# Four banks instead of two for a head's value tiles in the gated mixer and in retention

## What is computed

```python
q, k = silu(causal_dwconv(mq)), silu(causal_dwconv(mk))      # gated mixer only
# gated mixer, per head: a = decay weights exp(...) times (q . k) / 16
num_t = sum_{s<=t} a[t,s] * v[s]
den_t = max(|sum_{s<=t} a[t,s]|, exp(-m_t))
h_t   = num_t / den_t
hm    = sigmoid(mo) * head_rms(h)
# retention, per head:
o_t   = sum_{s<=t} gamma^(t-s) * (q_t . k_s) * v_s
hr    = silu(rg) * head_rms(o)
y     = gm * (hm @ w_mlstm_out) + gd * (hd @ w_diff_out) + gr * (hr @ w_ret_out)
```

## Time and profile before

| | |
|---|---|
| median of 3 runs | 2582.63 us (2580.34 to 2588.62) |
| the profiled execution | 2586.39 us, its span 2584.6 us |
| TensorE busy, share of the span | 2470.8 us, 96% |
| VectorE, ScalarE, GpSimd busy | 1088.5, 891.9, 186.5 us |
| mean granted TensorE clock | 0.976 of full |
| DMA | 219.96 MB, 85 GB/s |

### The profile page before, as it was taken

The page is one execution under the profiler, slowest core; times in us unless marked ns, Lnnn a source line. Parts: engine busy times, 40 slices in busy tenths (PEclk is TensorE's granted clock), DMA queues, the critical chain, the costliest instruction groups (busy, mean ns, idle before and its releaser), DMA issues.

```text
span 2584.6 us, 29079 instructions
## 1 busy us (share of the span) xinstructions
PE 2470.8 (96%) x11448; PEld 2021.8 (78%) x11448; DVE 1088.5 (42%) x1383; ACT 891.9 (35%) x1403; POOL 186.5 (7%) x252
## 2 busy tenths in 40 slices
PE   7999999999989999997999999999999999899997
PEld 7666788887877888886777788888877787788886
DVE  3444533445565443345444322223246534433334
ACT  3442422323443332234433423332245533522222
POOL 3000500002002200001000000000000000100001
PEclk9989999999989999998999999999999999999999
DMA  5611332232211323232222232222331123232221
GB/s 149 87 55 59 115 98 97 97 97 81 91 41 49 115 97 97 97 97 65 66 79 67 82 98 82 81 82 84 100 82 50 50 85 103 73 99 96 98 98 65
DMA packets 187040, 219.96 MB, mean 85 GB/s; under 512 B 20531, under 2 KB 141568, under 8 KB 186832
## 3 DMA queue, kind: packets, MB, share of 16 engines
q1 hardware_dynamic: 183200, 206.13, 25.2%
q0 software_dynamic: 3760, 12.73, 2.3%
HBM read 213.60 MB, written 5.24 MB: 85 GB/s over the span
## 4 chain that ended last, share of the span: by engine, by line
PE 91%; DVE 4%; ACT 2%; POOL 1%; issue 1%; DMA 0%; SPq 0%; POOLq 0%; ACTq 0%; DVEq 0%
PE A L471 46%; PE B L471 42%; DVE WL L1533 1%; DVE Y L1657 1%; ACT WH L1037 0%; DMA X<-in_x 0%; PE C L721 0%; ACT Y L1130 0%; ACT ar L1040 0%; PE C L946 0%; DVE st L1645 0%; POOL st L2137 0%; PE C L787 0%; POOL st L2123 0%; PE C L641 0%
## 5 line engine op out<-in xcount | busy, mean ns | idle before, releaser
L1533 DVE TENSOR_TENSOR WL<-RAW,WH 128x2048 fp32r<-128x2048 f32 (+1 forms) x197 | 450.4, 2286 | 753.1 <-ACT WH L1037 753.1
L1037 ACT ACTIVATE WH<-RAW 128x2048 fp32r<-128x2048 f32 (+1 forms) x197 | 376.0, 1909 | 666.9 <-PE A L471 601.7
L471 PE MATMUL B<-XH,WH 128*128 128x512 f32 x1360 | 538.6, 396 | 1.4 <-DVE XL L1543 1.4
L471 PE MATMUL B<-XL,WH 128*128 128x512 f32 x1360 | 531.6, 391 | 0.0
L471 PE MATMUL B<-XH,WL 128*128 128x512 f32 x1360 | 531.2, 391 | 0.0
L471 PE MATMUL A<-WH,YH 128*128 128x512 f32 (+1 forms) x976 | 377.8, 387 | 3.4 <-DVE YL L1592 1.8
L471 PE MATMUL A<-WL,YH 128*128 128x512 f32 (+1 forms) x976 | 377.1, 386 | 0.0
L471 PE MATMUL A<-WH,YL 128*128 128x512 f32 (+1 forms) x976 | 377.1, 386 | 0.0
L471 PEld LDWEIGHTS B<-XH,WH 128*128 128x128 f32 x1360 | 256.8, 189 | 70.4 <-issue 15.2
L471 PEld LDWEIGHTS B<-XH,WL 128*128 128x128 f32 x1360 | 256.6, 189 | 54.2
L471 PEld LDWEIGHTS B<-XL,WH 128*128 128x128 f32 x1360 | 257.0, 189 | 51.7
(11 more groups left out here) (272 smaller groups left out, 2106.4 us busy)
## 6 DMA issues: line engine op xcount, KB each, us to landing
RAW<-in_w_in SPq DMA_DIRECT2D x33, 1024.0 KB, 5.2
RAW<-in_mlp_w_up SPq DMA_DIRECT2D x32, 1024.0 KB, 5.4
RAW<-in_mlp_w_down SPq DMA_DIRECT2D x32, 1024.0 KB, 5.0
RAW<-in_w_in SPq DMA_DIRECT2D x48, 512.0 KB, 4.3
RAW<-in_w_ffn_in SPq DMA_DIRECT2D x22, 1024.0 KB, 5.0
RAW<-in_w_ffn_out SPq DMA_DIRECT2D x10, 1024.0 KB, 5.1
RAW<-in_mla_w_o SPq DMA_DIRECT2D x4, 1024.0 KB, 5.0
RAW<-in_swa_w_q SPq DMA_DIRECT2D x4, 1024.0 KB, 4.9
```

What stands on the lines that cost most here:

```text
L471: return nc.tensor.matmul(dst, l, r, start=first, stop=last)
L1037: nc.scalar.activation(WH[s][:, 0:n], RAW[s][:, 0:n], ACT.Copy).then_inc(hi_ready, 1)
L1533: tt(WL[s][:, 0:n], RAW[s][:, 0:n], f32(WH[s][:, 0:n]), ALU.subtract).then_inc(lo_ready, 1)
```

## The change

Two uses of B per head become uses of C. Tiles 0 and 1 stay in B0 and B1; tiles 2 and 3 go to the two C banks, and the two transposed tiles follow them in C. Since n0 is odd (85 and then 101), tile 2 gets C1 and tile 3 C0, and the transposed tiles C1 and C0, as before. ScalarE's drain and VectorE's copy of the denominator name the bank by the same function, and each frees the bank's own semaphore. A head now counts three uses of each B bank (before four) and two of each C bank (before one), so all wait numbers in the two stages change: the features that follow in B wait for tile 0's and tile 1's drain where they waited for tile 2's and tile 3's. The order of the instructions on every engine stays. The diff, cut to its core (the second PLAN line and the callers change in the same way):

```diff
-    ("ml", 16, 12, 32, 8, 4, 8),
+    ("ml", 16, 12, 24, 16, 4, 8),
-    ("ret", 16, 8, 32, 8, 4, 8),
+    ("ret", 16, 8, 24, 16, 4, 8),
+    def head_bank(name, t):
+        _, _, rb, n0, _, _ = BASE[name]
+        if t < 2:
+            return B[t], b_free[t], rb // 2 + 2, 3
+        u = n0 + t - 2
+        return C[u % 2], c_free[u % 2], u // 2, 2
+
+    def head_out(name, m):
+        u = BASE[name][3] + 2 + m
+        return C[u % 2], c_free[u % 2], u // 2, 2
...
-        def head_transposed(name, i, n0, src):
+        def head_transposed(name, i, src):
             pe.wait_ge(s_(name + "_h"), T * i + T)
             for m in range(2):
-                b = (n0 + m) % 2
-                pe.wait_ge(c_free[b], (n0 + m) // 2 + i)
+                bank, free, n, per = head_out(name, m)
+                pe.wait_ge(free, n + per * i)
                 for t in range(T):
-                    r = nc.tensor.transpose(C[b][:, tok(t)], src[:, t, tok(m)], ident[:])
+                    r = nc.tensor.transpose(bank[:, tok(t)], src[:, t, tok(m)], ident[:])
...
-        def decayed_values(name, i, rounds, rb, at, v, width):
+        def decayed_values(name, i, rounds, at, v, width):
             for t in range(T):
+                bank, free, n, per = head_bank(name, t)
                 pe.wait_ge(a_free[t], rounds)
-                b, u = t % 2, rb + 4 + t
-                pe.wait_ge(b_free[b], u // 2 + 4 * i)
+                pe.wait_ge(free, n + per * i)
                 for j in range(t + 1):
-                    r = mm(B[b][:, 0:width], at[:, j, (t - j) * P:(t - j) * P + P], v[:, j, 0:width], j == 0, j == t)
+                    r = mm(bank[:, 0:width], at[:, j, (t - j) * P:(t - j) * P + P], v[:, j, 0:width], j == 0, j == t)
...
-                features(c0 + 4 * i + 4, slot(c0), XH, XL, rb // 2 + 4 * i + 4)
+                features(c0 + 4 * i + 4, slot(c0), XH, XL, rb // 2 + 3 * i + 3)
...
-                    nc.scalar.activation(L_H[:, t, :], B[t % 2][:, 0:256], ACT.Copy, scale=stat(H_INV + t)).then_inc(b_free[t % 2], 1)
+                    nc.scalar.activation(L_H[:, t, :], bank[:, 0:256], ACT.Copy, scale=stat(H_INV + t)).then_inc(free, 1)
...
-                then(nc.vector.tensor_copy(den, B[t % 2][:, 256:257]))
+                then(nc.vector.tensor_copy(den, head_bank("ml", t)[0][:, 256:257]))
```

More of the change, by code:

```diff
@@ L815, in after_head @@
         def after_head(name, mix_name, i, ahead):
-            c0, _, rb, n0, _, _ = BASE[name]
+            c0, _, rb, _, _, _ = BASE[name]
             if ahead:
-                features(c0 + 4 * i + 4, slot(c0), XH, XL, rb // 2 + 4 * i + 4)
+                features(c0 + 4 * i + 4, slot(c0), XH, XL, rb // 2 + 3 * i + 3)
             else:
                 gate_chunk(mix_name, 0, 0)
-            head_transposed(name, i, n0, L_H)
+            head_transposed(name, i, L_H)
         def mlstm_head(i, ahead):
             c = c0 + 4 * i
-            features(c + 1, slot(c0 + 1), XH, XL, rb // 2 + 4 * i + 1)
+            features(c + 1, slot(c0 + 1), XH, XL, rb // 2 + 3 * i + 1)
             for j in range(2):
@@ L840, in mlstm_head @@
             scores("ml", i, ra + 3 * i + 2, L_Q, L_K)
-            decayed_values("ml", i, ra + 3 * i + 3, rb, L_A, L_V, 257)
+            decayed_values("ml", i, ra + 3 * i + 3, L_A, L_V, 257)
             after_head("ml", "mix0", i, ahead)
@@ L870, in retention_head @@
             for b in range(2):
-                pe.wait_ge(b_free[b], rb // 2 + 4 * i + 2)
+                pe.wait_ge(b_free[b], rb // 2 + 3 * i + 2)
             scores("ret", i, ra + 2 * i + 1, L_Q, L_K)
-            decayed_values("ret", i, ra + 2 * i + 2, rb, L_A, L_V, 256)
+            decayed_values("ret", i, ra + 2 * i + 2, L_A, L_V, 256)
             after_head("ret", "mix1", i, ahead)
@@ L1242, in head_rms, with head_hi @@
             for t in range(T):
+                bank, free, n, per = head_bank(name, t)
                 if inv:
                     act.wait_ge(s_(name + "_d"), T * i + t + 1)
-                    nc.scalar.activation(L_H[:, t, :], B[t % 2][:, 0:256], ACT.Copy, scale=stat(H_INV + t)).then_inc(b_free[t % 2], 1)
+                    nc.scalar.activation(L_H[:, t, :], bank[:, 0:256], ACT.Copy, scale=stat(H_INV + t)).then_inc(free, 1)
                 else:
                     act.wait_ge(s_(name + "_o"), T * i + t + 1)
-                    copy(L_H[:, t, :], B[t % 2][:, 0:256]).then_inc(b_free[t % 2], 1)
-                u = BASE[name][2] + 4 + t
-                act.wait_ge(b_free[t % 2], u // 2 + 1 + i * 4)
+                    copy(L_H[:, t, :], bank[:, 0:256]).then_inc(free, 1)
+                act.wait_ge(free, n + 1 + i * per)
                 nc.scalar.activation(xtmp[:, t // 2, 256 * (t % 2):256 * (t % 2) + 256], L_H[:, t, :], ACT.Square, scale=256 ** -0.5,
                                      accum_out=stat(H_SS + t)).then_inc(s_(name + "_ss"), 1)
-        def head_hi(name, i, n0):
+        def head_hi(name, i):
             for m in range(2):
                 act.wait_ge(s_(name + "_t"), 2 * i + m + 1)
-                copy(YH[:, ds(i * 2 + m, 1), :].rearrange("p a n -> p (a n)"), C[(n0 + m) % 2][:]).then_inc(s_(name + "_hi"), 1)
+                copy(YH[:, ds(i * 2 + m, 1), :].rearrange("p a n -> p (a n)"), head_out(name, m)[0][:]).then_inc(s_(name + "_hi"), 1)
         def head_tokens(i, func):
@@ L1312, in mlstm_head @@
                 after_conv(i + 1, 0)
-            head_hi("ml", i, n0)
+            head_hi("ml", i)
         act.wait_ge(s_("if_m"), 1)
@@ L1357, in retention_head @@
                 split(c0 + 6, 4, i)
-            head_hi("ret", i, n0)
+            head_hi("ret", i)
         split(c0 + 1)
@@ L1817, in values_by_token, with head_lo @@
                 stt(L_H[:, t, :], L_H[:, t, :], stat(H_R + t), L_O[:, t, :], ALU.mult, ALU.mult).then_inc(s_(name + "_h"), 1)
-        def head_lo(name, i, n0):
+        def head_lo(name, i):
             for m in range(2):
-                u = (n0 + m) % 2
+                bank, free, _, _ = head_out(name, m)
                 dve.wait_ge(s_(name + "_hi"), 2 * i + m + 1)
-                tt(YL[:, ds(i * 2 + m, 1), :].rearrange("p a n -> p (a n)"), C[u][:],
-                   f32(YH[:, ds(i * 2 + m, 1), :]).rearrange("p a n -> p (a n)"), ALU.subtract).then_inc(c_free[u], 1)
+                tt(YL[:, ds(i * 2 + m, 1), :].rearrange("p a n -> p (a n)"), bank[:],
+                   f32(YH[:, ds(i * 2 + m, 1), :]).rearrange("p a n -> p (a n)"), ALU.subtract).then_inc(free, 1)
         c0, ra, rb, n0, _, f0 = BASE["ml"]
@@ L1831, in convolution @@
             for m in range(2):
-                dve.wait_ge(b_free[m], rb // 2 + 1 + j + 4 * i)
+                dve.wait_ge(b_free[m], rb // 2 + 1 + j + 3 * i)
                 if j or m or not isinstance(i, int):
@@ L1863, in mlstm_head @@
                 convolution(i + 1, 0)
-            head_lo("ml", i, n0)
+            head_lo("ml", i)
         split(c0 + 2)
@@ L1921, in retention_head @@
             split(c0 + 6, 4, i)
-            head_lo("ret", i, n0)
+            head_lo("ret", i)
         split(c0 + 1)
```

## The result

The changed kernel takes 2565.26 us, the median of six runs (2562.64 to 2575.09), against 2582.64 us (2579.46 to 2588.62, six runs) for the kernel before. The ratio (changed to before) is 0.9934, with a 95% interval of 0.9921 to 0.9947. The forecast was 2566.0 us.

A forecast was written before the change was run, and what follows sets the result against it. TensorE, busy 96% of the span, was taken to bound the kernel. Idle time 10.4, slower clock 4.9 and restart 1.3 us gave 16.6 us off the 2582.6 us median: 2566.0 us, range 2562 to 2577.

The forecast's parts named there:

- The wait and its place: TensorE waits 10.4 us for tile 0's drain, all before the gated mixer's value matmuls in four heads; retention gains 0.
- The price of a block without the wait: Gated-mixer value blocks fall from 7.48, 9.14, 9.13 and 9.08 us to retention's 4.55 us, gaining 16.63 us.
- The clock: Gated-mixer heads 1 to 3 run at clock 0.81 behind the idle gap; without the gap 4.9 us go too.
- Rival A: Gated mixer: only the idle time goes, the lower clock stays; gain 11.7 us, 2570.9 us; chance 0.14.
- What is late next: Next head's query features in B0, heads 0 to 2, wait for tile 0's drain, in time by 0.06 us; cost 0.
- Rival B: Tile 0's drain comes later and next features stand still in heads 0 to 2; only 4.5 us stay, 2578.1 us; chance 0.09.
- Rival C: Cycling through four banks drops TensorE's clock more often, in retention too; slower, 2591.1 us; chance 0.02.
- Waits on C: Tiles 2 and 3 wait for C banks emptied some 28 us before head 1's tiles; worth nothing.
- Transposes: Transposes at the head's end wait for tiles 2 and 3 to be drained, with 7 us of cover; cost nothing.
- Loop arithmetic: Wait values climbing by 3 and 2 a head add instructions on TensorE's sequencer; bound 0.6 us, taken as 0.

The follow-up runs named there:

- retention alone: Changed kernel with the gated mixer put back to two banks, only retention using four: 2586.79 us, ratio 1.0002 to the kernel before.
- gated mixer alone: Changed kernel with retention put back to two banks, only the gated mixer using four: 2571.59 us, ratio 0.9942 to the kernel before.
- split behind: VectorE's weight split moved behind a gated-mixer head's four denominators: 2574.18 us in the kernel before (two banks), 2565.69 us in the changed kernel (four banks).
- half gap: Changed kernel, but gated-mixer tile 2 also waits for VectorE's split of a weight chunk, idle 1.28 us in heads 0 to 2: 2571.46 us, ratio 0.9946.
- later drain: Changed kernel with two unused VectorE instructions ahead of tile 0's denominator in each gated-mixer head: 2572.59 us, ratio 0.9957.
- three banks: Changed kernel, but gated-mixer tile 3 waits for tile 1's drain, so only tile 2 is free: 2583.99 us, ratio 0.9985.
- old waits: Four banks as in the changed kernel, but tiles 2 and 3 still wait for the drains of tiles 0 and 1: 2585.33 us, ratio 0.9999.

## Why the prediction was right

**The wait and its place.** Only the gated mixer's four heads had something to win: retention alone gives 1.0002, the gated mixer alone the whole gain in the middle part.

**The price of a block without the wait.** Read off retention as 4.55 us, it is 4.57 to 4.59. The sum was 16.63 us; the blocks give 16.5 and the middle part 16.46. The parts are confirmed one by one: 10.4 us of idle time; 0.25 to 0.31 us of restart for each gap where the sum had 0.33 (split behind: 0.64 us idle, block 5.53 - 4.58 = 0.95; half gap: 1.28 and 1.53); and the lower clock, 9.14 - 7.49 = 1.65 us between two heads with the same gap (retention alone).

**The clock.** Rival A was given 0.14, since head 0 had kept its clock in spite of the gap. The experiments set the gap and count the heads:

| idle before a value tile or the features | heads that lost the clock |
|---|---|
| none (changed kernel twice, gated mixer alone, split behind) | 0 of 16 |
| 0.64 us (two banks, split behind) | 0 of 4 |
| 0.77 us (later drain) | 0 of 3 |
| 1.28 us | 0 of 4 |
| 2.20 us (three banks) | 2 of 4 |
| 2.60 us (before, retention alone, old waits) | 9 of 12 |
| 3.50 us | 4 of 4 |

In these blocks the loss follows the length of the gap. Each length but those of none and of 2.60 us rests on one profile, so the shares are rough. Which heads are hit changes from one execution to the next (1, 2, 3; 0, 1, 3; 0, 2, 3), so head 0 of the profile before was one that got away, not a head of another kind. My forecast took three of four for granted, the count of a single profile, and had luck that two further ones gave the same count. The Trainium skill ("TensorE: Matmul & The Clock Gate", section "Why this matters for your kernels") blames longer gaps than 2.60 us; here 2.20 us were enough in two heads of four, so the measurement decides.

The length of a gap isn't the whole rule, as gaps in parts that no edit touches show in the same twelve profiles. Two of them in the kernel before, each with the stretch behind it; directly ahead of both gaps the clock was 1.00:

```profile
133.21 0.98 PE L641 MATMUL C<-ident,ar 128*128 128x128 f32 x7 [1.36 <-ACT ar L1040]
133.21:137.21 4.00, 3.31 (x10) 1.92 (x11) 1.39 (x4) 2.98 (x4) 0.00 (x0) 0.63 0.00 0
...
1225.82 1.27 PE L777 MATMUL C<-ident,ar 128*128 128x128 f32 x8 [2.15 <-ACT ar L1317]
1225.82:1231.82 6.00, 6.00 (x24) 4.99 (x25) 3.24 (x3) 3.91 (x4) 0.00 (x0) 0.72 0.00 0
```

The gap of 2.15 us lost the clock in 3 of 12 profiles; the 512-wide products behind it then start 0.43 us apart instead of 0.23. Of 122 gaps of 0.4 to 1.6 us that stood alone, with no other of 0.4 us or more within some 10 us, none did, which fits the table. But the gap of 1.36 us before the transposes of line 641, which comes four times in the first block and which a gap of 0.69 us follows some 2 us later, lost it in 32 of 48 cases. What makes that place worse, the second gap or the kind of work around it, is not shown: no experiment set it.

**What is late next.** The small reserve was real, 0.08 us where the forecast had 0.06: free of cost as it stands (the split behind in four banks gains nothing), and nearly every further delay of the drain comes through (1.12 of 1.20 us). Rival B's mechanism exists; the change just doesn't meet it.

**The costs taken as nothing.** Waits on C: no entry. Transposes: in head 0 the last scaled tile ended at 1281.58 + 0.48 = 1282.06 us, the first transpose came at 1288.6, so 6.5 us of cover were left of 7:

```profile
1281.58 0.48 DVE L1830 SCALAR_TENSOR_TENSOR ar<-ar,st 128x256 f32<-128x256 f32 x1 [0.45 <-POOL st L2203]
...
1288.55 1.03 PE L800 MATMUL C<-ident,ar 128*128 128x128 f32 x8
```

Loop arithmetic: no cost in the blocks. Rival C: no clock below 1.00 in any retention block of any profile, and four banks with the old waits give 0.9999. The Trainium skill's section "A second HAM failure mode: psum-queue depth-cycling", on the same page, tells of another kernel, whose clock swung; nothing of the kind shows in the retention blocks here.

**The size.** -0.64% was forecast and -0.66% measured. The interval alone (0.9921 to 0.9947, from 14 to 20 us) couldn't have told the forecast from rival A with much force; the shortened gap and the blocks' clock did.

## What to carry to other kernels

Price a wait on a matmul engine by the whole stretch around it, from the last instruction ahead of it to one that runs steadily behind, and against a neighbour that has no wait: here 10.4 us of shown idle time stood for 16.5 us. Before spending banks, look at what the drain itself waits for: moving one line of another engine's stream gave 12.7 of the 16.5 us with the banks as they were. A partial remedy may only move the gap: with three banks it stood one tile later, and 13.2 of the 16.5 us remained.

## What was not expected of the hardware

Idle gaps of 2.2 us were enough to bring the granted clock from 2.4 to 1.2 GHz in two heads of four, while gaps of 1.28 us did in none of four. Elsewhere in the same kernels a gap of 1.36 us with another close behind it was followed by the lower clock in 32 of 48 cases, so a length that was harmless in one place need not be so in another. The slow stretch costs about 1.65 us each time and hits different heads in different executions; with a gap of 2.6 us it hit three heads in each of three profiles. The part of the kernel ahead of the mixer, which no experiment touched, varied by almost 10 us between profiles (1263.50 to 1273.30), which is more than half of the effect under study. The gap of 1.36 us of line 641 has a share in that: in the profile with the shortest such part it cost the clock in one head of four, in the one with the longest in all four.
